# First transfers issued from two queues, and slab 0's rounded part multiplied ahead of the turns of tiles 2 and 3

## The reference, cut to what matters

```python
def reference(x, ...):
    for layer in range(DEPTH):          # DEPTH = 2
        if layer % 2 == 0:
            h = conv_sgu_mixer(x, ...)  # begins with h = x @ w_in, 1024 x 2048
        else:
            h = dilated_attention_mixer(x, ...)
        x = layer_norm(DN_ALPHA * x + h, ...)
        x = layer_norm(DN_ALPHA * x + swiglu(x, ...), ...)
```

## Time and profile before

| | us |
|---|---|
| three runs | 1411.33, 1412.48, 1413.11 |
| median | 1412.48 |
| the profiled execution | 1411.54 |
| its span (first to last instruction) | 1409.7 |
| TensorE busy | 1393.7 |
| GpSimd, VectorE, ScalarE busy | 633.5, 500.8, 491.9 |

### The profile page before, as it was taken

The page is one execution under the profiler, slowest core; times in us unless marked ns, Lnnn a source line. Parts: engine busy times, 40 slices in busy tenths (PEclk is TensorE's granted clock), DMA queues, the critical chain, the costliest instruction groups (busy, mean ns, idle before and its releaser), DMA issues.

```text
span 1409.7 us, 17172 instructions
## 1 busy us (share of the span) xinstructions
PE 1393.7 (99%) x6695; PEld 1186.2 (84%) x6695; DVE 500.8 (36%) x702; ACT 491.9 (35%) x742; POOL 633.5 (45%) x295
## 2 busy tenths in 40 slices
PE   8999999999999999999999999999999999999997
PEld 7887888888888889888898888899898888888886
DVE  4996511111140036777334666633051111110003
ACT  4465532232322253333332433333263222322123
POOL 5884544444444444444543324333254444444443
PEclk9999999999999999999999999999999999999999
DMA  9232233333433223333322222332223333343221
GB/s 281 84 103 86 67 105 104 91 103 89 135 93 103 91 69 95 90 90 90 95 85 79 74 88 71 95 120 75 60 61 114 95 102 92 93 130 104 90 75 60
DMA packets 175326, 134.75 MB, mean 96 GB/s; under 512 B 4213, under 2 KB 157577, under 8 KB 175272
## 3 DMA queue, kind: packets, MB, share of 16 engines
q1 hardware_dynamic: 175272, 133.98, 31.7%
HBM read 131.87 MB, written 2.10 MB: 95 GB/s over the span
## 4 chain that ended last, share of the span: by engine, by line
PE 95%; DVE 2%; ACT 2%; POOL 1%; DMA 1%; issue 0%; SPq 0%; DVEq 0%; ACTq 0%
PE pq L572 19%; PE pq L573 19%; PE pq L574 19%; PE pq L594 7%; PE pq L596 7%; PE pq L595 7%; PE pq L900 3%; PE pq L901 3%; PE pq L902 3%; PE pq L878 1%; PE pq L838 1%; PE pq L851 1%; DVE pq L1292 1%; PE pq L871 1%; ACT xt_lo L1003 1%; PE pq L608 1%
## 5 line engine op out<-in xcount | busy, mean ns | idle before, releaser
L498 POOL TENSOR_TENSOR w_lo<-w_stage,w_hi 128x1024 fp32r<-128x1024 f32 x236 | 567.5, 2410 | 730.5 <-ACT w_hi L988 730.4
L572 PE MATMUL pq<-xt_hi,w_hi 128*128 128x512 f32 (+1 forms) x1272 | 479.9, 377 | 0.1
L573 PE MATMUL pq<-xt_lo,w_hi 128*128 128x512 f32 (+1 forms) x1272 | 476.5, 375 | 0.0
L574 PE MATMUL pq<-xt_hi,w_lo 128*128 128x512 f32 (+1 forms) x1272 | 476.4, 375 | 0.0
L988 ACT ACTIVATE w_hi<-w_stage 128x1024 fp32r<-128x1024 f32 x236 | 245.6, 1053 | 254.5 <-PE pq L596 184.7
L572 PEld LDWEIGHTS pq<-xt_hi,w_hi 128*128 128x128 f32 x1272 | 239.6, 188 | 44.4 <-DVE xt_lo L1281 1.1
L574 PEld LDWEIGHTS pq<-xt_hi,w_lo 128*128 128x128 f32 x1272 | 239.5, 188 | 42.9
L573 PEld LDWEIGHTS pq<-xt_lo,w_hi 128*128 128x128 f32 x1272 | 239.7, 188 | 41.9
L1523 DVE TENSOR_TENSOR hidden<-pq,hidden 128x512 f32<-128x512 f32 x44 | 30.4, 692 | 369.4 <-PE pq L574 369.4
L594 PE MATMUL pq<-w_hi,ht_hi 128*128 128x512 f32 x352 | 137.1, 389 | 0.0
L596 PE MATMUL pq<-w_hi,ht_lo 128*128 128x512 f32 x352 | 136.9, 389 | 0.0
(11 more groups left out here) (185 smaller groups left out, 1329.1 us busy)
## 6 DMA issues: line engine op xcount, KB each, us to landing
w_stage<-in_od_w_qkv_dram SPq DMA_DIRECT2D x72, 512.0 KB, 3.8
w_stage<-in_ffn_w_gate_dram SPq DMA_DIRECT2D x44, 512.0 KB, 3.8
w_stage<-in_ffn_w_up_dram SPq DMA_DIRECT2D x44, 512.0 KB, 3.9
w_stage<-in_ffn_w_down_dram SPq DMA_DIRECT2D x44, 512.0 KB, 3.4
w_stage<-in_ev_w_in_dram SPq DMA_DIRECT2D x16, 512.0 KB, 6.0
w_stage<-in_ev_w_out_dram SPq DMA_DIRECT2D x8, 512.0 KB, 3.3
w_stage<-in_od_w_out_dram SPq DMA_DIRECT2D x8, 512.0 KB, 3.3
x_res<-in_x_dram SPq DMA_DIRECT2D x4, 512.0 KB, 6.0
```

What stands on the lines that cost most here:

```text
L498: pool.tensor_tensor(w_lo[slab % RING][:, :], w_stage[slab % RING][:, :], w_hi[slab % RING][:, :].bitcast(F32), ALU.subtract).then_inc(w_l ...
L572: pe.matmul(ps[bank][:, at], hi[:, k, :], xt_hi[:, k, at], start=(k == 0), stop=False)
L573: pe.matmul(ps[bank][:, at], hi[:, k, :], xt_lo[:, k, at], start=False, stop=False)
L574: last = pe.matmul(ps[bank][:, at], lo[:, k, :], xt_hi[:, k, at], start=False, stop=(k == KD - 1))
```

## The change

SP no longer transfers the identity, x1 and the second half of x0: it begins with the first half of x0 (512 columns, 256 KB, a new semaphore `x_half`), then slab 0, x2, x3 and slabs 1 to 3. The ACT queue issues the identity, the second half of x0 and x1 before ScalarE does anything else. The first four turns of x0 wait for `x_half` and the identity, the other four for `x_loaded[0]`.

On TensorE the 24 matmuls of slab 0 on tiles 0 and 1 are cut apart. Behind the turns of x0 and x1 it waits for `xt_set` 4 and `w_hi_ready` 1 and runs the 16 with the rounded slab (L624, L625 of the changed kernel). Then come the turns of x2 and x3, and then, behind `w_lo_ready` 1, the 8 with the remainder (L630). The 24 of tiles 2 and 3 follow as before. All of them add up in the same bank. The order on ScalarE (but for its three issues), VectorE and GpSimd is as before.

```diff
--- before.py
+++ after.py
@@ -186,6 +186,7 @@
         w_lo_ready = sem("w_lo_ready")
         w_used = sem("w_used")
         x_loaded = [sem(f"x_loaded{i}") for i in range(TILES)]
+        x_half = sem("x_half")
         ident_loaded = sem("ident_loaded")
         rot_loaded = sem("rot_loaded")
         wsp_loaded = sem("wsp_loaded")
@@ -421,11 +422,10 @@
                     sp.dma_start(dst[:, :], src[layer, which:which + 1, :].partition_broadcast(P)
                                  ).then_inc(ln_loaded[e], 16)
 
-            sp.dma_start(ident[:, :], ident_in).then_inc(ident_loaded, 16)
-            for i in range(TILES):
+            sp.dma_start(x_res[:, 0, 0:512], x[0, 0:P, 0:512]).then_inc(x_half, 16)
+            load(0)
+            for i in range(2, TILES):
                 sp.dma_start(x_res[:, i, :], x[0, i * P:(i + 1) * P, :]).then_inc(x_loaded[i], 16)
-                if i == 1:
-                    load(0)
             for slab in range(1, RING):
                 load(slab)
             sp.dma_start(par_rows[0:CONV_WIDTH, 0:CONV_CH], ev_conv_w[0]).then_inc(par_loaded, 16)
@@ -599,9 +599,13 @@
 
                 for half in range(2):
                     bank = turn_bank(e, i, half)
-                    if e and i < SHIFT_TILES:
+                    if e == 0 and i == 0 and half == 0:
+                        pe.wait_ge(x_half, 16)
+                    elif e == 0:
+                        pe.wait_ge(x_loaded[i], 16)
+                    elif i < SHIFT_TILES:
                         pe.wait_ge(x_normed, 2 * ((e - 1) * SHIFT_TILES + i) + half + 1)
-                    elif e:
+                    else:
                         pe.wait_ge(x_normed_end, 2 * (e - 1) + half + 1)
                     for c in range(4):
                         col = (4 * half + c) * P
@@ -610,13 +614,20 @@
 
 
             pe.wait_ge(ident_loaded, 16)
-            for i in range(TILES):
-                pe.wait_ge(x_loaded[i], 16)
-                turn_x(0, i)
+            turn_x(0, 0)
+            turn_x(0, 1)
 
             pe.wait_ge(xt_set, 4)
+            pe.wait_ge(w_hi_ready, 1)
+            first_hi, first_lo = (w[0][:, :].rearrange("p (k n) -> p k n", n=P) for w in (w_hi, w_lo))
+            for k in range(KD):
+                pe.matmul(ps[0][:, 0:2 * P], first_hi[:, k, :], xt_hi[:, k, 0:2 * P], start=(k == 0), stop=False)
+                pe.matmul(ps[0][:, 0:2 * P], first_hi[:, k, :], xt_lo[:, k, 0:2 * P], start=False, stop=False)
+            turn_x(0, 2)
+            turn_x(0, 3)
             slab_ready(0)
-            columns(0, 0, (0, 2))
+            for k in range(KD):
+                pe.matmul(ps[0][:, 0:2 * P], first_lo[:, k, :], xt_hi[:, k, 0:2 * P], start=False, stop=(k == KD - 1))
 
             def turn_parameters():
 
@@ -1038,6 +1049,9 @@
                 high(2)
                 high(3)
 
+            act.dma_start(ident[:, :], ident_in).then_inc(ident_loaded, 16)
+            act.dma_start(x_res[:, 0, 512:D_MODEL], x[0, 0:P, 512:D_MODEL]).then_inc(x_loaded[0], 16)
+            act.dma_start(x_res[:, 1, :], x[0, P:2 * P, :]).then_inc(x_loaded[1], 16)
             act.wait_ge(ones_set, 2)
 
             act.activation(std[:, 0:1], eps[:, 0:1], ACT.Copy)
```

## The result

| | median us | runs | range |
|---|---|---|---|
| before | 1412.71 | 7 | 1411.33 to 1413.12 |
| changed | 1417.52 | 7 | 1416.77 to 1418.32 |

The ratio is 1.0034, 95% interval 1.0025 to 1.0044: slower by 4.8 us. The profiled execution took 1417.51 with a span of 1415.7. I had forecast 1414.2 with a range of 1411.0 to 1416.4 and most of the chance on "within 0.2%". The sign of the sum was right, its size (1.7 us) was about a third of what came, and the time lies outside the range.

A forecast was written before the change was run, and what follows sets the result against it. TensorE, busy 99%, bounds the kernel, so slab 1's start sets the end: 0.4, 1.6 and 0.3 us less, 1.0, 1.9 and 1.1 more, +1.7 on the median 1412.48, gives 1414.2; range 1411.0 to 1416.4.

The forecast's parts named there:

- Where x1 lands: Start, ACT's queue: x1, sharing the engines with slab 0, lands at 6.8 us (6.4 to 7.7), against 6.7 before.
- T: End of TensorE's turns of x1: forecast 8.7 us, range 7.8 to 9.6, against 9.08 before.
- Where the first half lands: Start: x0's first half lands at 4.5 us (3.9 to 4.7), turning starts 0.9 earlier, the second half follows in time.
- The wait ahead of the moved matmuls: TensorE behind x1's turns: idle 1.65 us for ScalarE's rounded slab 0, in place of 0.65.
- The clock on the moved matmuls: The 16 moved matmuls run at the lower level, 0.24 us each, 3.8 in all; the clock rises about 3.9 after their start.
- Rival A: The clock rises soon after the moved matmuls start; slab 1 starts at 19.3, no change, 1412.5 us; chance 0.20.
- VectorE behind the turns: Behind the turns of x2 and x3 TensorE waits for VectorE's halves of x3: new idle time of 1.1 us.
- Nothing absorbs the shift: Behind slab 1's start: nothing found that absorbs a shift, so the end moves by the same amount.
- The sum: All terms up to slab 1: its start moves from 19.3 to 21.0, +1.7 us, giving 1414.2.
- Rival C: x1 lands at 7.7 and the clock stays low through the turns of x2 and x3: +3.7 us, 1416.2; chance 0.12.

The follow-up runs named there:

- e8: The changed kernel, but SP issues x2 and what follows only when x1 has landed; median 2.9 us above that of before.
- e3: The changed kernel with x1 issued by SP between the first half of x0 and slab 0; median 2.1 us above that of before.
- e4: Transfers as in e3, TensorE's order as in the kernel before; median 0.1 us below that of before.
- e10: e4 with 8 and 4 constant matmuls added, before the first turns and behind x1's; median 0.4 us below that of before.
- e1: TensorE's new order alone, with the transfers of the kernel before; median 1.3 us above that of before.
- e7: The changed kernel with x1 and slab 0 exchanged between the queues (x1 on SP, slab 0 on ACT); median 4.6 us above that of before.
- e2: The changed kernel's transfers alone, with TensorE's order as before; median 2.4 us above that of before.
- e6: e1 with 20 and 8 constant matmuls added, before the first turns and behind x1's; median 1.0 us above that of before.
- e12: The changed kernel with constant matmuls added: 8 before the first turns, 10 between x0's and x1's, 4 behind x1's; median 2.1 us above that of before.
- e5: The kernel before with 20 and 8 constant matmuls added, before the first turns and behind x1's; median 0.7 us above that of before.
- e9: The kernel before with 10 and 4 constant matmuls added, before the first turns and behind x1's; median 1.4 us below that of before.
- e11: e1 with 10 and 4 constant matmuls added, before the first turns and behind x1's; median 0.9 us below that of before.

## Why the prediction was wrong

**Where x1 lands: wrong, and this is the step that failed.** The forecast had x1 landed at 6.8 (6.4 to 7.7) and T at 8.7; it landed at 9.6, and T was 11.55. I counted the bytes that have to move before x1 is there as identity, x0, x1 and at most an equal share of slab 0: 1638 KB at the worst. The changed SP row has x2 right behind slab 0 and issues it 0.01 us ahead of x1; I did not count it. x1 and x2 moved half and half from 6 to 8 us. With x2 the count is 2162 KB, which on my own curve, with 1932 KB at 8.0, is about 8.6, and landing at 9.1 (an estimate); 9.6 was measured, with x3 beside x1's last rows. e8 takes x2 and x3 away and x1 lands at 7.6, the worst end of my range. So 2.0 of the 2.8 us are the tiles of x that I left out. The other 0.8 are the choice of 6.8 within the range. I gave as its reason that x moves more bytes than a slab beside it. From 4 to 5 us that was so, but the x there was the second half of x0: slab 0 had moved whole by 5.9, before x1 had well begun, so x1 paid for all of it.

**Where the first half lands: nearly right.** Turns began at 4.17 (4.5 forecast, 3.9 to 4.7). But what released them was the identity, whose landing on ACT's queue (0.75 + 3.4) I had not worked out; the half of x0 was there at 3.9 (0.74 + 3.2). That the second half would follow in time was wrong: 0.63 of waiting. It costs nothing beside the late x1, but in e3, e4 and e10 it is what keeps T at 9.1 to 9.3.

**The wait ahead of the moved matmuls: right.** 1.72 in the changed kernel and in e1, against 1.65 forecast.

**The clock on the moved matmuls: right in kind.** They ran 0.21 apart (0.24 assumed), 3.55 us in all. I let the clock rise 3.9 us behind their start. By the time that the 16 turns took, it rose about 3.9 behind it in e1 and about 5.0 in the changed kernel, which there gave 2.4 us of turns in place of 1.9. Rival A, with the moved matmuls at the upper level, did not occur in the changed kernel, e1, e7 or e8. It did in e3, where the clock rose before them, and the two groups of e1's runs make it likely for half of those. So that the clock came late was not certain from the kernel, and the forecast has some luck in it here.

**VectorE behind the turns: right.** 0.78 (1.1 forecast); 0.95 in e1.

**Nothing absorbs the shift: right.** Slab 1's 4.86 us and the medians' 4.8 agree, as they do for e2, e4, e6, e8 and e12 within 0.2 and for e10 within 0.3. For e1, e3, e5, e7, e9 and e11 one profile and the median differ by 0.3 to 1.6 us, in both directions.

**The sum.** From T to slab 1 I forecast 12.3 us; it took 12.6. Nearly all of the miss is T, 2.85 of 3.15 us. That the rest agrees so well is in part luck: the moved matmuls were 0.25 shorter than forecast and the wait for VectorE 0.3, the turns behind them 0.5 longer. Rival C had the right form, with x1 at 7.7 and the clock late, and even it stopped short at 1416.2, since its x1 came from the same count. Its chance of 0.12, and the 0.15 for slower, were too low for the same reason: the byte count was treated as a bound although it left out a transfer that the order of the issues shows.

**What the change would have needed.** Not only x1 in time: with x1 on SP (e3) or the clock up (e11), the new order still does not beat the old one (e4, e9); counted from T it is 0.5 us behind in both pairs. The old order uses the time in which ScalarE and GpSimd prepare slab 0 for the turns of x2 and x3. The new order waits for ScalarE instead, and saves the wait for GpSimd that the turns had hidden: 13.11 against turns to 13.41.

## What to carry to other kernels

When a transfer is moved to a second queue, list for each moment what stands at the head of both queues and count all of it ahead of the transfer that is waited for, down to the one issued with it; look at the lengths of the rows too: beside rows of 4 KB on SP's queue a slab with rows of 512 bytes took 10.5 us to land from ACT's, against 5.1 from SP's queue in the changed kernel. A matmul that waits for a shorter chain is no gain where other useful work had already covered the longer one. And what is put behind an idle stretch at the start of a kernel may run at the lower clock, which here cost 3.0 of the 4.86 us (e12). Where an effect turns on when the clock rises, one profile is not enough: read it beside the spread of the runs.

## What the runs showed of the hardware that I had not expected

- Two queues do not share the engines by bytes. In e7 they moved about equal counts of rows in each stretch read, whether the rows were 4 KB or 512 bytes, and the short rows got an eighth of the bytes. In the changed kernel the counts were 300 of 512 bytes against 117, nearly all of 2 KB. No run separates what decides this.
- The moment of the clock's rise varies more than I took it to. Read from the starts of the single matmuls, it came 3.1 us behind the first added matmul in e11, 3.6 in e12, 3.7 in e5, 4.4 in e6 and 6.1 in e9, though all began at 1.00 us; in e10 it came at 9.9 us. In e2 24 turns in a row took 5.38 us, all at the lower level; in e3 it rose 0.1 us behind 12 turns of 2.8 us. I have no rule for it from these runs.
- The granted clock is printed as 1.00 from the first microsecond on, also where the durations say the lower level (the turns of before, the moved matmuls of e1). The trace's entries for it begin only with the first rise (13.7 us before, 14.7 in e1, 18.2 in the changed kernel), and these moments agree with the durations. Where it falls in the course of the run, as in e7, the column shows it.
- A recurring 1.1 us in the second layer, described above, comes and goes with the execution. What decides it stays open.
